# One tail as guest of the front parts, four tails behind the last front part with one loading of their weights

## The chip, the cores and the metric

One core of a Trainium2 chip runs the kernel. The metric is the device time of one execution in microseconds (us); of several runs the median stands. Matrix work runs on TensorE (PE; PEld is its loading of weights), elementwise work with reductions on VectorE (DVE), functions and copies on ScalarE (ACT), gathers are issued by GpSimd (POOL) and plain transfers by SyncE (SP). All transfers run on the same 16 DMA engines, here called the bus.

## The reference

One layer over 1024 tokens of 1024 features, all in float32:

```python
h = rmsnorm(x, norm_mix)
proj = h @ w_in                                    # parts for two token mixers
x = x + (g_gla * y_gla + g_swa * y_swa) @ w_out    # gated mixers, sliding window and linear attention
x = x + peer_ffn(rmsnorm(x, norm_ffn), ...)        # 8 heads x 16 of 16384 experts for each token
ple_gate = sigmoid(rmsnorm(x, norm_ple) @ w_ple_gate)
x = x + ple_gate * (p @ w_ple_proj)                # p: 256 features a token
return rmsnorm(x, norm_final)
```

In `peer_ffn` each head's query scores two lists of 128 keys; the 16 best pairs pick 16 experts. Of each expert a row u (1024) gives a dot product with the token, and, weighted by gelu of that and a softmax share, a row v (1024) is added up.

## The kernel before

The tokens are 8 tiles of 128. Three kinds of work run at once, woven by a plan of steps:

- **Rows.** Each tile has 8 heads x 16 experts = 128 rows. A row is one gather by GpSimd (line 596): for each of 128 tokens the u and v of its expert, 8 KB, 1 MB in all, into one of NS = 10 slots of the ring `uv`. VectorE takes the dot product (line 1354), ScalarE makes the weight (lines 1094, 1099), then either VectorE adds the weighted v (line 1382) or ScalarE makes a diagonal (line 1108) and TensorE adds it up in `ysum` (line 837); then the slot is free for the gather ten rows on. Step n (0 to 511) takes rows 2n and 2n + 1; every engine's program is a loop over the same steps and does its work in that order. From step 384 on (tiles 6 and 7) TensorE takes 3 of 4 rows, in tiles 3 to 5 every second; the first six rows of each tile are VectorE's. The top-16 searches of later heads run on VectorE 12 steps ahead.
- **Front parts.** SEGS = (1, 1, 2, 2, 2) tiles: norm, projections, mixers, output projection and queries of a segment, before its rows. Their weights are pieces of 1 MB (`slabs` in DRAM), loaded in order of use into a ring of RS = 3 places (`slab`, line 513), each when the piece three before has been used. The stages wq0 to wq8 are the queries (wq0 to wq7 use a piece each); with wq1 to wq8 VectorE runs `largest`, the 16 best of 128 for two lists of each tile.
- **Tails.** The per-layer embedding, the final norm and the output of a group of tiles, GROUPS = ((0, 1), (2, 3), (4, 5), (6,), (7,)). Stages: T0 (read-in of the tiles, sums of squares), gn (gain row), T1 (scale and turn), pg0 to pg3 (gate, one piece each), pp (embedding, one piece), mx, T2 (last norm, output). A tile's row sums are built in `acc[i % 2]`; when its rows are done, SyncE stores it to DRAM (`x2_d`, line 577), and T0's read-in (line 548) fetches the group back into `bufA`. Only the last tile's tail works in place, in `acc`.

The order is the list PLAN. `closing(s)` follows the last front stage of segment s with its queries wq2 to wq8, at `pace` steps each, woven with the opening of the next segment or with a tail: HOST = {0: 3, 1: 4} says that tail 0 is a guest of segment 3, and tail 1 of segment 4. So before, steps are: wq0 368, wq1 370, T0 of tail 1 at 372, wq2 374, then wq3 to wq8 every four steps to 400 with pg0 to pg3 and pp of tail 1 at 382 to 398 between them, T2 at 404; tail 2 from 407 to 425, tail 3 from 452 to 470, tail 4: pp 496, gn 498, the rest behind the rows, 514 to 521. SyncE issues all plain transfers in the order of the plan and waits, in that order, for what each needs; it runs ahead of the other engines as far as those waits let it.

Of the kernel before, what the change touches and what calls it, by code (L numbers as in the profile page):

```python
# [16 lines left out]
KT = D // P  # L17
# [18 lines left out]
TT = max(SEGS)  # L36
# [26 lines left out]
HOST = {0: 3, 1: 4}  # L63
# [67 lines left out]
def plan():  # L131

    found = []

    def stand(of, n, step):
        at = {name: at for at, o, name in found if o == of}
        step = max(step, found[-1][0] if found else step, at.get(BEHIND.get(n), step - 1) + 1)
        found.append((step, of, n))

    for s in range(NSEG):  # L140
        names = front_names(s)
        if not s or s - 1 in GUEST:
            names = OPENING + names
        due = DUE[s]
        last = len(names) - 1
        begin = found[-1][0] + 1 if found else due - last
        for i, n in enumerate(names):
            if n is not None:
                stand(s, n, begin + i * (due - begin) // last)
        pace = 2 if s in GUEST else 1 if s else 0.5  # L150
        for i, (of, n) in enumerate(closing(s)):
            stand(of, n, due + math.ceil(pace * (i + 1)))
    for q, tiles in enumerate(GROUPS):
        if q == LAST_GROUP:

            stand(q, "pp", PER_TILE * NTILE - 16)
            stand(q, "gn", PER_TILE * NTILE - 14)
            for i, n in enumerate(n for n in TAIL if n not in ("pp", "gn")):
                stand(q, n, END + 2 + i)
        elif q not in HOST:  # L160
            begin = max(found[-1][0] + 3, PER_TILE * (tiles[-1] + 1) + 4)
            for i, n in enumerate(TAIL):
                stand(q, n, begin + 2 * i)
    return found
# [110 lines left out]
for _, _s, _name in PLAN:  # L275
    if has_vector_part(_s, _name):
# [3 lines left out]

LOADS = [((s, n), n, USES_END[s, n] - (len(token_banks(SEGS[s])) if n[:2] == "wq" and n != "wq0" else 0))
         for _, s, n in PLAN if n in PIECES]
# [18 lines left out]
def build(nc, a, out):  # L301
    with ExitStack() as ctx:
# [59 lines left out]
        tp = [by_token_tile(bufC if q == LAST_GROUP else bufQ) for q in range(len(GROUPS))]  # L362
# [35 lines left out]
        x2 = [acc[:, (NTILE - 1) % 2:(NTILE - 1) % 2 + 1, :] if q == LAST_GROUP else x1 for q in range(len(GROUPS))]  # L398
# [62 lines left out]
        tail_out = sem("tail_out")  # L461

# [36 lines left out]
        def _(sp):  # L499
# [20 lines left out]
            def after_stage(at, s, n):  # L520
# [15 lines left out]
                if at == 0 and n == ("pp" if s == LAST_GROUP else "T0"):  # L536
                    tiles_of = GROUPS[s]
                    t0, tt = tiles_of[0], len(tiles_of)
                    if s in HOST:
                        sp.wait_ge(x1_out, 16 * WRITES[HOST[s] + 1])  # L540
                        sp.wait_ge(tile_set, SETS[HOST[s] + 1])
                        sp.wait_ge(vec_done, VEC_ORDER[HOST[s], "rt"])
                    else:
                        sp.wait_ge(tail_out, 16 * s)
                    if s != LAST_GROUP:
# [3 lines left out]
                    if s in HOST:  # L549
                        sp.wait_ge(bank_full, USES_END[HOST[s], f"va{last_batch(HOST[s])}"])  # L550
                    sp.dma_start(tpT[:, :, 0:tt * P], a["pT"][:, :, t0 * P:(t0 + tt) * P]).then_inc(tp_in, 16)
                    sp.dma_start(g_fin[0:1, :], a["g_fin"].unsqueeze(0)).then_inc(gfin_in, 16)
                if at == 2 and n == "T2":
# [12 lines left out]
            for n in range(FIRST, LAST + 3):  # L566
# [8 lines left out]
                if at == 0 and 1 <= i < NTILE:  # L575
# [26 lines left out]
        def _(pe):  # L602
# [17 lines left out]

            def turned(src, f0, tt):
# [20 lines left out]
            def by_token(src, tt):  # L642
                w = next_piece()
# [65 lines left out]
            def stage(s, n):  # L709
# [103 lines left out]
                elif kind == "pg":  # L813
                    if c == 0:
                        emptied_through(s, "T1")
                    by_token(thT, tt)
                elif n == "pp":
                    w = next_piece().rearrange("p k n -> p (k n)").rearrange("p (k n) -> p k n", k=2)
# [39 lines left out]
        def _(act):  # L858
# [77 lines left out]
            def stage(s, n):  # L936
# [120 lines left out]
                elif n == "T0":  # L1057
                    if s == LAST_GROUP:
                        act.wait_ge(x2_done, NTILE)
                    else:  # L1060
                        act.wait_ge(x2_in, 16 * (s + 1))
# [434 lines left out]
```

## Time and profile before

| | us |
|---|---|
| median of 3 runs | 3462.57 |
| lowest, highest | 3459.61, 3462.61 |
| the profiled execution, its own time | 3464.53 |
| its span, first to last instruction | 3462.6 |
| TensorE busy | 2831.6 (82%) |
| VectorE busy | 2525.6 (73%) |
| ScalarE, GpSimd busy | 1412.9 (41%), 1287.2 (37%) |
| moved by DMA | 1368.17 MB, mean 395 GB/s |

The shares are means over stages with different limits; they don't say which engine a stage waits for. Stretches are given in us from the span's start. A line of the timeline is start, duration, engine, line, what it writes and reads, and in brackets the engine's idle time before it with what ended it.

### The profile page before, as it was taken

To read this page: it belongs to the slowest core of one execution; us is meant where nothing else is said; L and a number is where in the kernel's file an instruction comes from. 1 tells how busy PE (TensorE), PEld (TensorE's weight loads), DVE (VectorE), ACT (ScalarE), POOL (GpSimd) and SP (SyncE) were. 2 spreads that over 40 slices of the span, in tenths; PEclk is the share of its full clock that TensorE was granted. 3 is DMA by queue.
4 is the path that set the end of the run, shared out by engine and by line. 5 is a ranking of instruction groups with operands and counts; after the bars stand their busy time and mean duration, and the time that the engine had idled before them with its cause. 6 is when DMAs were issued, how large, how long until landed. Compare 5 with 4: busy or idle time off the path is not lost.

```text
span 3462.6 us, 35613 instructions
## 1 busy us (share of the span) xinstructions
PE 2831.6 (82%) x11300; PEld 1912.9 (55%) x11300; DVE 2525.6 (73%) x5340; ACT 1412.9 (41%) x3593; POOL 1287.2 (37%) x1028
## 2 busy tenths in 40 slices
PE   8879769998978998876877969987896978758675
PEld 7877557765656865543644637655564645224223
DVE  0147658888878878788687996788778895776664
ACT  2324434445524344454343443444434444334332
POOL 0012223343442344443453443343334343544441
PEclk9999789999999999987988989999998998878887
DMA  7579999999999999999999999999999999999995
GB/s 243 201 302 419 370 383 421 421 421 420 420 419 388 392 421 421 420 412 414 411 422 409 411 400 421 421 421 417 399 410 420 413 399 418 408 421 422 421 422 213
DMA packets 193630, 1368.17 MB, mean 395 GB/s; under 512 B 22154, under 2 KB 24074, under 8 KB 29732
## 3 DMA queue, kind: packets, MB, share of 16 engines
q0 software_dynamic: 147456, 1073.81, 75.0%
q1 hardware_dynamic: 45988, 292.09, 21.2%
q8 instruction: 92, 1.51, 0.2%
q14 instruction: 94, 0.77, 0.1%
HBM read 1356.37 MB, written 9.44 MB: 394 GB/s over the span
## 4 chain that ended last, share of the span: by engine, by line
PE 37%; DMA 35%; DVE 12%; issue 7%; ACT 6%; POOL 2%; DVEq 0%; another core or an unknown queue 0%; POOLq 0%; SPq 0%; ACTq 0%
DMA uv<-in_uv,idx 30%; PE bank L639 12%; PE bank L649 11%; PE ysum L837 9%; DMA slab<-in_slabs 4%; DVE acc L1382 3%; DVE uv L1354 3%; POOL uv L596 2%; PE bank L706 1%; DVE lidx L1210 1%; ACT bufX L913 1%; DVE vals L1207 1%; DMA out<-bufA 1%; ACT dots L1099 1%; DVE bufE L1204 1%
## 5 line engine op out<-in xcount | busy, mean ns | idle before, releaser
L596 POOL DMA_INDIRECT uv<-in_uv,idx x1024 | 1287.0, 1257 | 2118.9 <-PE ysum L837 944.6
L1354 DVE SCALAR_TENSOR_TENSOR uv<-uv,hbuf 128x1024 f32<-128x1024 f32 x1024 | 1246.3, 1222 | 476.8 <-DMA uv<-in_uv,idx 457.2
L837 PE MATMUL ysum<-uv,diag 128*128 128x512 f32 x2092 | 1098.3, 670 | 373.2 <-ACT diag L1108 369.6
L837 PEld LDWEIGHTS ysum<-uv,diag 128*128 128x128 f32 x2092 | 427.0, 213 | 919.3 <-ACT diag L1108 471.1
L1382 DVE SCALAR_TENSOR_TENSOR acc<-uv,dots,acc 128x1024 f32<-128x1024 f32 x501 | 641.3, 1280 | 59.3 <-ACT dots L1099 42.3
L1094 ACT ACTIVATE dots<-dots 128x2 f32<-128x2 f32 x512 | 103.0, 201 | 1049.0 <-DVE uv L1354 1044.6
L639 PE MATMUL bank<-bufA,slab 128*128 128x256 f32 (+1 forms) x2400 | 439.9, 343 | 10.0 <-DMA slab<-in_slabs 9.4
L639 PEld LDWEIGHTS bank<-bufA,slab 128*128 128x128 f32 x2400 | 390.7, 195 | 72.6 <-issue 25.3
L649 PE MATMUL bank<-slab,bufA 128*128 128x256 f32 x1408 | 318.6, 385 | 5.7 <-DMA slab<-in_slabs 3.3
L649 PEld LDWEIGHTS bank<-slab,bufA 128*128 128x128 f32 x1408 | 270.6, 193 | 60.3 <-issue 16.4
L639 PE MATMUL bank<-bufC,slab 128*128 128x256 f32 (+1 forms) x1280 | 244.7, 353 | 21.4 <-ACT bufC L870 10.4
L1099 ACT ACTIVATE dots<-dots,gexp 128x1 f32<-128x1 f32 x1024 | 246.0, 287 | 20.6
L639 PEld LDWEIGHTS bank<-bufC,slab 128*128 128x128 f32 x1280 | 217.2, 203 | 61.2 <-issue 23.9
L1094 ACT ACT_TABLE_LOAD x160 | 205.3, 1283 | 2.9
L1108 ACT ACTIVATE diag<-ident,dots 128x128 f32<-128x128 f32 x523 | 196.6, 395 | 18.2 <-PE ysum L837 11.2
L870 ACT ACTIVATE bufE<-bank 128x512 f32<-128x512 f32 (+1 forms) x146 | 75.5, 523 | 289.1 <-PE bank L639 273.3
L649 PE MATMUL bank<-slab,bufC 128*128 128x256 f32 x512 | 120.5, 395 | 27.7 <-DVEq L1281 15.1
L649 PEld LDWEIGHTS bank<-slab,bufC 128*128 128x128 f32 x512 | 101.4, 199 | 50.5 <-DVEq L1281 16.7
L649 PE MATMUL bank<-slab,bufQ 128*128 128x256 f32 x512 | 120.9, 397 | 4.6 <-DMA slab<-in_slabs 3.9
L639 PE MATMUL bank<-bufQ,slab 128*128 128x256 f32 (+1 forms) x640 | 115.0, 338 | 7.8 <-DMA slab<-in_slabs 7.0
L649 PEld LDWEIGHTS bank<-slab,bufQ 128*128 128x128 f32 x512 | 102.4, 201 | 29.1 <-issue 7.3
L639 PE MATMUL bank<-bufB,slab 128*128 128x256 f32 (+1 forms) x640 | 118.4, 344 | 0.0
(160 smaller groups left out, 2303.6 us busy)
## 6 DMA issues: line engine op xcount, KB each, us to landing
slab<-in_slabs SPq DMA_DIRECT2D x255, 1024.0 KB
uv<-in_uv,idx POOLq DMA_INDIRECT x1024
x_d<-acc SPq DMA_DIRECT2D x7, 512.0 KB, 7.9
bufA<-in_x SPq DMA_DIRECT2D x3, 1024.0 KB, 11.6
bufA<-x_d SPq DMA_DIRECT2D x3, 1024.0 KB
out<-bufA SPq DMA_DIRECT2D x3, 1024.0 KB
bufQ<-in_x SPq DMA_DIRECT2D x2, 1024.0 KB, 16.6
x_d<-bufA SPq DMA_DIRECT2D x3, 512.0 KB, 7.7
```

What stands on the lines that cost most here:

```text
L596: nc.gpsimd.indirect_dma_start(out=uv[:, at % NS, :], out_offset=None, in_=a["uv"], in_offset=bass.IndirectOffsetOnAxis(ap=idx[:, g % 4, k ...
L639: m = mm(o, w[:, k, g * P:g * P + P], src(k), start=(k == 0), stop=(k == KT - 1))
L649: m = mm(b[:, c0:c0 + PW], src[:, k, t * P:t * P + P], w[:, k, :], start=(k == 0), stop=(k == KT - 1))
L706: m = mm(b[:, :, q], of[:, t, g * HD:g * HD + HD], pT[:, :, q], start=True, stop=True)
L837: ins = mm(ysum[:, c, :], diag[:, m % DS, :], uv[:, at % NS, D + c * 512:D + c * 512 + 512], start=(m == first), stop=(m == last))
L870: fn(dst, src, kw.pop("func", ACT.Copy), **kw).then_inc(emptied, 1)
L913: fn(probs[:, j, :], probs[:, j, :], ACT.Exp, bias=sm[:, 1, j:j + 1], accum_out=sm[:, 3, j:j + 1]).then_inc(window_exp, 1)
L1094: fn(part, part, ACT.Gelu_apprx_tanh).then_inc(gelu_done, 1)
L1099: m = fn(dots[:, g % 3, k:k + 1], dots[:, g % 3, k:k + 1], ACT.Copy, scale=gexp[:, g % 4, k:k + 1])
L1108: fn(diag[:, m % DS, :], ident[:], ACT.Copy, scale=dots[:, g % 3, k:k + 1]).then_inc(diag_done, 1)
L1354: v.scalar_tensor_tensor(out=row, in0=row, scalar=1.0, in1=hbuf[:, i % HB, :], op0=ALU.mult, op1=ALU.mult, accum_out=dots[:, g % 3, k:k + ...
L1382: v.scalar_tensor_tensor(out=row, in0=uv[:, at % NS, D:2 * D], scalar=dots[:, g % 3, k:k + 1], in1=row, op0=ALU.mult, op1=ALU.add).then_in ...
```

## The change

Tail 1 is no longer a guest of segment 4; the queries wq2 to wq8 of segment 4 follow each other every two steps, 372 to 384. Tail 1 runs after them, T0 at 387 to T2 at 405, pieces at 393 to 401; tail 2 runs from 408 to 426; tails 3 and 4 keep their steps. The five pieces of the tails (pg0 to pg3, pp) are loaded for tail 0 through the ring as before, and then once more, when the queries are done, into places that are free from then on: the three places of `slab`, `bufE` and `bufC`. Tails 1 to 4 use them from there. Tile 6, the only tile of its group, works in place in `acc` as tile 7 did, and is not stored to DRAM and read back. The last tail's embedding goes to the second half of `bufB` in place of `bufC`. The ring's list LOADS shrinks from 255 pieces to 235.

```diff
--- before.py
+++ after.py
@@ -60,7 +60,7 @@
 
 
 GROUPS = ((0, 1), (2, 3), (4, 5), (6,), (7,))
-HOST = {0: 3, 1: 4}
+HOST = {0: 3}
 GUEST = {h: q for q, h in HOST.items()}
 TAIL = ["T0", "gn", "T1", "pg0", "pg1", "pg2", "pg3", "pp", "mx", "T2"]
 LAST_GROUP = len(GROUPS) - 1
@@ -147,7 +147,7 @@
         for i, n in enumerate(names):
             if n is not None:
                 stand(s, n, begin + i * (due - begin) // last)
-        pace = 2 if s in GUEST else 1 if s else 0.5
+        pace = 2 if s in GUEST or s == NSEG - 1 else 1 if s else 0.5
         for i, (of, n) in enumerate(closing(s)):
             stand(of, n, due + math.ceil(pace * (i + 1)))
     for q, tiles in enumerate(GROUPS):
@@ -278,8 +278,14 @@
         VEC_ORDER[_s, _name] = _n
 
 
+FIRST_KEPT = len(HOST)
+KEPT = ["pg0", "pg1", "pg2", "pg3", "pp"]
+
+DIRECT = [q for q, tiles in enumerate(GROUPS) if len(tiles) == 1]
+
+
 LOADS = [((s, n), n, USES_END[s, n] - (len(token_banks(SEGS[s])) if n[:2] == "wq" and n != "wq0" else 0))
-         for _, s, n in PLAN if n in PIECES]
+         for _, s, n in PLAN if n in PIECES and not (n in KEPT and s >= FIRST_KEPT)]
 
 MOVED = [i for i in range(NTILE) if i not in AT]
 BATCHES = [sum(2 * t for t in SEGS[:s]) for s in range(NSEG + 1)]
@@ -359,7 +365,8 @@
         sqT = by_feature_tile(bufQ)
         yswT = by_feature_tile(bufQ)
         thT = by_feature_tile(bufQ)
-        tp = [by_token_tile(bufC if q == LAST_GROUP else bufQ) for q in range(len(GROUPS))]
+        tp = [by_token_tile(bufB)[:, 1:TT, :] if q == LAST_GROUP else by_token_tile(bufQ) for q in range(len(GROUPS))]
+        kept = [*(slab[:, i, :] for i in range(RS)), bufE[:], bufC[:]]
         HALF = 512 * TT
         loga = bufE[:, 0:HALF].rearrange("p (t n) -> p t n", t=TT)
         zs = bufE[:, HALF:2 * HALF].rearrange("p (t n) -> p t n", t=TT)
@@ -395,7 +402,7 @@
         uv = sb("uv", [P, NS, 2 * D])
         hbuf = sb("hbuf", [P, HB, D])
         acc = sb("acc", [P, 2, D])
-        x2 = [acc[:, (NTILE - 1) % 2:(NTILE - 1) % 2 + 1, :] if q == LAST_GROUP else x1 for q in range(len(GROUPS))]
+        x2 = [acc[:, tiles[0] % 2:tiles[0] % 2 + 1, :] if q in DIRECT else x1 for q, tiles in enumerate(GROUPS)]
         diag = sb("diag", [P, DS, P])
         vals = sb("vals", [P, LS, NH, 2, TOPK])
         lidx = sb("lidx", [P, LS, NH, 2, TOPK], U32)
@@ -459,6 +466,7 @@
         tp_in = sem("tp_in")
         gfin_in = sem("gfin_in")
         tail_out = sem("tail_out")
+        kept_in = [sem(f"kept_in{i}") for i in range(len(KEPT))]
 
         firsts = [(ident[:], a["ident"]), (g_mix[:], a["g_mix"])]
         consts = [(wga[:], a["wga"]), (wa2[:], a["wa2"]), (chunk_of[:], a["chunk_of"]), (tri[:], a["tri"]),
@@ -536,20 +544,28 @@
                 if at == 0 and n == ("pp" if s == LAST_GROUP else "T0"):
                     tiles_of = GROUPS[s]
                     t0, tt = tiles_of[0], len(tiles_of)
-                    if s in HOST:
-                        sp.wait_ge(x1_out, 16 * WRITES[HOST[s] + 1])
-                        sp.wait_ge(tile_set, SETS[HOST[s] + 1])
-                        sp.wait_ge(vec_done, VEC_ORDER[HOST[s], "rt"])
-                    else:
+                    host = HOST.get(s, NSEG - 1)
+                    if s <= FIRST_KEPT:
+
+                        sp.wait_ge(x1_out, 16 * WRITES[host + 1])
+                        sp.wait_ge(tile_set, SETS[host + 1])
+                        sp.wait_ge(vec_done, VEC_ORDER[host, "rt"])
+                    if s > 0:
                         sp.wait_ge(tail_out, 16 * s)
-                    if s != LAST_GROUP:
+                    if s not in DIRECT:
                         for t in tiles_of:
                             sp.wait_ge(x2_out[t % 2], 16 * (t // 2 + 1))
                         sp.dma_start(x2[s][:, 0:tt, :], x2_d[t0:t0 + tt].rearrange("t p d -> p t d")).then_inc(x2_in, 16)
-                    if s in HOST:
-                        sp.wait_ge(bank_full, USES_END[HOST[s], f"va{last_batch(HOST[s])}"])
+                    if s <= FIRST_KEPT:
+                        sp.wait_ge(bank_full, USES_END[host, f"va{last_batch(host)}"])
                     sp.dma_start(tpT[:, :, 0:tt * P], a["pT"][:, :, t0 * P:(t0 + tt) * P]).then_inc(tp_in, 16)
                     sp.dma_start(g_fin[0:1, :], a["g_fin"].unsqueeze(0)).then_inc(gfin_in, 16)
+                if at == 2 and (s, n) == (NSEG - 1, f"wq{NH}"):
+
+                    sp.wait_ge(bank_full, USES_END[s, n])
+                    sp.wait_ge(vec_done, VEC_ORDER[s, n])
+                    for place, name, landed in zip(kept, KEPT, kept_in):
+                        sp.dma_start(place, a["slabs"][PIECES.index(name)]).then_inc(landed, 16)
                 if at == 2 and n == "T2":
                     sp.wait_ge(vec_done, VEC_ORDER[s, "T2"])
                     t0, tt = GROUPS[s][0], len(GROUPS[s])
@@ -572,7 +588,7 @@
                         sp.wait_ge(x2_out[i % 2], 16 * (i // 2))
                     sp.dma_start(acc[:, i % 2, :], x1_d[i]).then_inc(acc_in[i % 2], 16)
                 i, at = divmod(n - 3, PER_TILE)
-                if at == 0 and 1 <= i < NTILE:
+                if at == 0 and 1 <= i <= GROUPS[DIRECT[0]][0]:
                     sp.wait_ge(x2_done, i)
                     sp.dma_start(x2_d[i - 1], acc[:, (i - 1) % 2, :]).then_inc(x2_out[(i - 1) % 2], 16)
                 for at in range(3):
@@ -618,6 +634,13 @@
                 pe.wait_ge(slab_in[n % RS], 16 * (n // RS + 1))
                 return slab[:, n % RS, :].rearrange("p (k n) -> p k n", k=KT)
 
+            def tail_piece(s, n):
+                if s < FIRST_KEPT:
+                    return next_piece()
+                i = KEPT.index(n)
+                pe.wait_ge(kept_in[i], 16)
+                return kept[i].rearrange("p (k n) -> p k n", k=KT)
+
             def turned(src, f0, tt):
                 for f in range(f0, f0 + 4, 2):
                     for gs in feature_banks(tt):
@@ -639,8 +662,8 @@
                             m = mm(o, w[:, k, g * P:g * P + P], src(k), start=(k == 0), stop=(k == KT - 1))
                     m.then_inc(bank_full, 1)
 
-            def by_token(src, tt):
-                w = next_piece()
+            def by_token(src, tt, w=None):
+                w = next_piece() if w is None else w
                 for ts in token_banks(tt):
                     b = bank_for()
                     for t in ts:
@@ -813,9 +836,9 @@
                 elif kind == "pg":
                     if c == 0:
                         emptied_through(s, "T1")
-                    by_token(thT, tt)
+                    by_token(thT, tt, tail_piece(s, n))
                 elif n == "pp":
-                    w = next_piece().rearrange("p k n -> p (k n)").rearrange("p (k n) -> p k n", k=2)
+                    w = tail_piece(s, n).rearrange("p k n -> p (k n)").rearrange("p (k n) -> p k n", k=2)
                     pe.wait_ge(tp_in, 16 * (s + 1))
                     for q in range(2):
                         for t in range(tt):
@@ -1055,8 +1078,8 @@
                     for q in range(2):
                         copied(row[:, q * 512:q * 512 + 512], full())
                 elif n == "T0":
-                    if s == LAST_GROUP:
-                        act.wait_ge(x2_done, NTILE)
+                    if s in DIRECT:
+                        act.wait_ge(x2_done, GROUPS[s][0] + 1)
                     else:
                         act.wait_ge(x2_in, 16 * (s + 1))
                     square_sums(junk_t0, [(x2[s][:, t, :], stat_t[:, 0, t:t + 1]) for t in range(tt)])
```

## Rows read from the trace of the kernel before

**Rows 1.** the profile page: DMA queues, with packets, MB and share of the 16 engines' span

```profile
q0 software_dynamic: 147456, 1073.81, 75.0%
q1 hardware_dynamic: 45988, 292.09, 21.2%
```

**Rows 2.** busy us (and records) of PE, PEld, DVE, ACT, POOL in a stretch, PEclk, DMA share, GB/s

```profile
2623.10:2729.80 106.70, 86.80 (x314) 58.85 (x313) 88.31 (x250) 42.18 (x106) 44.77 (x35) 0.87 1.01 419
2729.80:2756.80 27.00, 20.78 (x79) 15.07 (x78) 26.44 (x71) 8.89 (x24) 9.99 (x8) 0.94 0.99 397
2756.80:2837.80 81.00, 72.38 (x237) 42.47 (x235) 69.27 (x194) 33.70 (x86) 33.75 (x30) 0.99 0.98 398
2837.80:2974.00 136.20, 103.35 (x297) 57.41 (x298) 92.98 (x173) 69.95 (x165) 57.86 (x44) 0.87 1.00 410
2974.00:3239.60 265.60, 178.58 (x362) 77.12 (x361) 183.98 (x347) 99.62 (x272) 118.34 (x99) 0.83 1.01 421
3239.60:3413.00 173.40, 122.71 (x216) 47.56 (x214) 117.80 (x214) 51.95 (x169) 81.46 (x65) 0.84 1.01 422
...
2878.90:2959.90 81.00, 80.44 (x262) 48.06 (x262) 55.72 (x104) 43.31 (x104) 40.82 (x31) 1.00 0.99 405
1081.00:1107.00 26.00, 25.69 (x105) 17.02 (x104) 25.16 (x97) 12.90 (x32) 10.03 (x9) 1.00 1.01 409
1112.40:1130.70 18.30, 18.30 (x75) 14.41 (x74) 13.13 (x47) 2.71 (x10) 3.75 (x4) 0.91 0.81 300
```

**Rows 3.** stretches again, only line 1354 (dot products): DVE busy (records)

```profile
2623.10:2729.80 106.70, 39.21 (x64) 0.87 1.01 419
2756.80:2837.80 81.00, 34.23 (x56) 0.99 0.98 398
```

**Rows 4.** timeline of SP and PE: tile 6's store, the last tail's pieces; start, us, instruction

```profile
3092.72 0.32 SPq L577 DMA_DIRECT2D x_d<-acc  x1
...
3435.90 16.29 PE L649 MATMUL bank<-slab,bufQ 128*128 128x256 f32 x64 [0.72 <-ACT bufQ L899]
...
3441.86 0.33 SPq L513 DMA_DIRECT2D slab<-in_slabs  x1
```

**Rows 5.** line 1207 (MAX8 of the queries' scores) in 2623.1 to 2729.8

```profile
L1207 DVE MAX8 vals<-bufE x32: 273/276/296, 2636.1 to 2728.2; 128x8 f32<-128x128 f32 x32
```

**Rows 6.** timeline of DVE, one call of `largest` and what follows

```profile
1088.75 0.86 DVE L1207 MAX8 vals<-bufE 128x8 f32<-128x128 f32 x4
...
1094.23 1.23 DVE L1354 SCALAR_TENSOR_TENSOR uv<-uv,hbuf 128x1024 f32<-128x1024 f32 x1 [0.18 <-DVE lidx L1210]
```

**Rows 7.** timeline of SP: the read-ins of tails 1 and 2, the store of tile 5

```profile
2617.75 0.38 SPq L548 DMA_DIRECT2D bufA<-x_d  x1
...
2736.01 0.33 SPq L577 DMA_DIRECT2D x_d<-acc  x1
...
2856.40 0.37 SPq L548 DMA_DIRECT2D bufA<-x_d  x1
```

**Rows 8.** timelines of ACT, DVE and POOL around T0 of tail 2; in brackets the idle time

```profile
2867.72 1.06 ACT L877 ACTIVATE bufQ<-bufA 128x1024 f32<-128x1024 f32 x1 [14.47 <-DMA bufA<-x_d]
...
2871.68 0.17 DVE L1143 RECIPROCAL stat_t<-stat_t 128x2 f32<-128x2 f32 x1 [15.25 <-ACT stat_t L881]
...
2876.05 1.36 POOL L596 DMA_INDIRECT uv<-in_uv,idx  x1 [20.79 <-PE ysum L837]
```

**Rows 9.** DMA queues in 2870 to 2880, columns as in rows 1

```profile
q1 hardware_dynamic: 564, 3.26, 79.8%
q0 software_dynamic: 118, 0.83, 21.5%
```

**Rows 10.** groups of PE in 2883.4 to 2951.6: busy us, mean ns, idle before

```profile
L837 PE MATMUL ysum<-uv,diag 128*128 128x512 f32 x73 | 32.5, 592 | 0.0
L649 PE MATMUL bank<-slab,bufQ 128*128 128x256 f32 x128 | 28.3, 379 | 0.0
```

## The prediction

> **What bounds the kernel now.** I read the page's queue table first, then busy time by stretch, then the timeline around single events. The two DMA queues together keep the 16 engines busy for 96% of the span [rows 1], and where nothing is in the way the bus moves 422 GB/s (stretch F below, [rows 2]). One gather or one weight load is 1,048,576 bytes, so 2.49 us of bus; a step has two gathers, 4.97 us. Adding bytes would cost time almost everywhere, but the bus is not the only limit near the front parts: over steps 391 to 427 it moves 398 and 410 GB/s (C and D below, [rows 2]), and in 2878.9 to 2959.9, where a tail of two tiles runs alone, TensorE is busy for 80.4 of 81.0 us [rows 2]. The question for each load removed is therefore whether the bus or something else sets the pace where it stood.
>
> I cut the time after step 370 into stretches whose edges are starts of dot products, two per step: A steps 370 to 385, B 386 to 390, C 391 to 404, D 405 to 427, E 428 to 475, F 476 to 509, then the last tail. The count in [rows 3] confirms the steps: each dot product leaves two records, so x64 is 16 steps.
>
> **Bytes.** Before, five tails load five pieces each, 25 loads. After, ten: five for the guest, five kept. Fifteen loads fewer: five of tail 2 (all in D), five of tail 3 and three of tail 4 in E, one of tail 4 in F, one behind the last gather. That last one is hidden: it is issued at 3441.86 under a run of TensorE that goes from 3435.90 for 16.29 us without a gap [rows 4], so I price it at 0; were TensorE to wait for it, it would be 2.5. Tile 6 also no longer goes out to DRAM (0.5 MB at 3092.72 [rows 4]) and back (a tail's read-in, half the size): 2.5 us of bus, in E.
>
> **E and F.** TensorE works 178.6 of 265.6 us and 122.7 of 173.4, VectorE 184.0 and 117.8 [rows 2], so the bus decides and bytes turn into time: E loses eight loads (19.9) and 2.5, so 22.4 us; F loses 2.5. If the shorter tails meet a little idle time of the bus, E gives 19.
>
> **A: the queries of the last front part, now one every two steps.** Before, A holds four calls of `largest` for two tiles: 32 MAX8, eight each [rows 5]. After, wq1 to wq8 all fall there, eight calls. One call takes 5.3 us of VectorE (from the first MAX8 at 1088.75 to 1094.05, 0.18 before the next dot product at 1094.23, [rows 6]). VectorE's work in A goes from 88.3 [rows 2] to 88.3 + 4 x 5.3 = 109.5 us, against a bus need of 16 x 4.97 + 6 x 2.49 = 94.5 and TensorE, which gives up two pieces and some turning of the guest tail and takes three pieces of queries at 7.1 us [rows 10] with their score products, some 93. VectorE becomes the bound. The nearest row where queries of two tiles come every two steps is 1081.0 to 1107.0: four steps in 26.0 us, VectorE at 25.16, 97% [rows 2]. So A takes 109.5 / 0.97 = 113, and 114 with the first pair of steps, where no landed rows are in store yet: +7.3 against 106.7. Bounds 109.5 (no idle time) and 120 (a wait for ScalarE of 1 us in each of seven stages besides).
>
> **B: the burst, and the wait for the residual rows.** SyncE now issues the five kept loads only when VectorE has done wq8 (step 385), then waits for `x2_done` 6, stores tile 5 and only then reads in tiles 2 and 3 for tail 1. Before, that read-in left at 2617.75, four steps ahead of T0 [rows 7]; nobody waited for it. In front of it now stand 5 x 2.49 + 1.25 us and its own 2.49: 16.2 us of bus. The ring of ten rows is full of landed rows at the end of A (VectorE was the slow one), and lets only four more gathers out before ScalarE stands at T0: 10.0 us. All of it is bus-bound, so the rows land some 26 us after the first dot product of step 386. From the landing the trace has a case, T0 of tail 2: ScalarE goes on at 2867.72 after 14.47 us of waiting, VectorE at 2871.68 after 15.25, GpSimd issues its next gather at 2876.05 after 20.79 [rows 8], and the dot product two steps later that begins the row of 81.0 us stands at 2878.9, 11.2 behind the landing. So 26 + 1 + 11 = 38 us for B, against 27.0: +11. What is queued behind ScalarE's wait: the weights of rows 776 on, their diagonals, so TensorE's sums, so the slots of the ring. Bounds: 29 if the gathers stand behind the whole burst and the ring's store hides more of it (16.2 + 1 + 11.2), and 45 if each byte ahead of the read-in shares the bus with a gather (2 x 16.2 + 1 + 11.2).
>
> On such sharing, the Trainium skill's page "DMA: Bandwidth & Descriptors" (section on queues, rings and completion order) says that each engine takes turns between the rows of queues that have work, a packet at a time; by it B would lie at its upper bound, 45, and the whole sum at -2, if gathers never ran out. In the trace a side that has nothing to send leaves the bus to the other: in 2870 to 2880 q1 has 79.8% and q0 21.5% [rows 9]. My sum goes by what is there to be moved.
>
> **C: tail 1 alone.** Its twin in the trace is tail 2, 2878.9 to 2959.9: the same instructions on two tiles with the same three rows in two steps on TensorE, 81.0 us for 14 steps, TensorE 80.4. In its dense part, 2883.4 to 2951.6, the four pieces cost TensorE 28.3 us, 7.1 each, and the row sums 32.5 [rows 10]. The bus would need 14 x 4.97 = 69.6. So C is TensorE's: I take 80, against 81.0 before, though two loads fewer are in it. Bounds 74 (the ring lets dot products run two rows further ahead and the next stall absorbs it) and 82.
>
> **D: tail 2.** Five loads fewer are 12.4 us of bus. But three of them filled a hole: during T0's wait gathers stop, and from 2870 to 2880 q0 moves 0.83 MB where the bus could move 4.2 [rows 9]; the missing 3.4 MB are 8 us. The wait itself hangs on a store and a read-in, which stay. The other two stood where TensorE is saturated. I take 134.5 against 136.2; bounds 125 (the loads' 12.4 nearly whole) and 137.
>
> **Sum.** A +7.3, B +11.0, C -1.0, D -1.7, E -22.4, F -2.5, end 0: -9.3 us. The profiled execution took 3464.5, of which 3462.6 are span; it becomes 3455.2. The median of the runs is 3462.57, so 3453.3.
>
> **Rivals.** (1) *The bus sets the time everywhere.* Then A to C keep their bytes and D gives all: 22.4 + 2.5 + 12.4 = 37.3, median 3425. For it: the bus at or near 1.0 in every row of [rows 2]. Against it: VectorE's 109.5 us of work in A, and TensorE's row of 81.0. The skill's "Perfetto Trace Analysis" (Identifying the Most-Contended Engine) holds that matmul busy time is a bad metric and weight loads' busy share a good one; by it TensorE would have room in C and D, which is this rival. The trace shows 48.1 of 81.0 for the weight loads in that row, yet the matmuls follow each other with 0.6 us of gaps, so I give it 0.12. (2) *Half way:* the ring absorbs more of TensorE's backlog, C 74 and D 127: 13.5 us better, median 3440. 0.18. (3) *The burst costs more:* B 45 and A 119 make -9.3 + 7 + 5 = +2.7, median 3465, no change that can be told. 0.20. (4) *Slower: the stages of queries are paced by the chain of TensorE, ScalarE and VectorE,* not by VectorE's work. Place: steps 372 to 385, each wq waiting for its copies. Price: steps 123 and 124, where TensorE is crowded by pieces, took 18.3 us with VectorE only 13.1 of it busy [rows 2]; seven pairs at 18.3 in place of 14.2 are +29, median 3482. It decides from 16.5 us a pair on ((9.3 + 6.9) / 7 above 14.2). Against it: 1081.0 to 1107.0, with no wait in it. 0.08. (5) That the loads are not saved: the counts in the code say 255 before and 235 plus five after; no chance of its own.
>
> **Numbers.** Forecast 0.42. A measurement of this kernel can tell about 0.2%, 6.9 us, from no change, and my forecast lies only 2.4 us beyond that: two thirds of its chance are faster, one third the same. Faster: 0.12 + 0.18 + 0.27 = 0.57; same 0.15 + 0.17 = 0.32; slower 0.08 + 0.03 = 0.11. The range 3432 to 3472 takes in the forecast with its bounds and rivals 2 and 3, and leaves out 1 and 4, 0.20.
>
> **What would show it.** In the changed profile: 64 MAX8 between the dot products of steps 370 and 386 and VectorE at 95% or more there, in 114 us; a wait of ScalarE for the read-in of tiles 2 and 3 of about 10 us (step 388), with hardly a gather moving behind it; TensorE at 99% while tail 1 runs, with a bus below 370 GB/s; a hole of some 8 us after T0 of tail 2; and E shorter by 22. The prediction is wrong if VectorE has room in A, if tail 1 runs at 5 us a step, or if E gives less than 19.

## The result and the profile after

The changed kernel takes 3467.14 us, median of 18 runs, against 3461.89 for the kernel before, also of 18. The ratio is 1.0019 with a 95% interval of 1.0012 to 1.0027, so some 6.6 us slower; in a second set of runs (after_again below) it was 1.0013 (1.0000 to 1.0025), 4.5 us. I had forecast 3453.3, 9.3 us faster. The time lies inside the stated range of 3432 to 3472, but the sign is the other.

The page of the kernel after, against [rows 1] and the table ahead of the prediction:

```profile
span 3465.2 us, 35599 instructions
...
DMA packets 191182, 1351.40 MB, mean 390 GB/s; under 512 B 21882, under 2 KB 23802, under 8 KB 29204
...
q0 software_dynamic: 147456, 1073.81, 75.4%
q1 hardware_dynamic: 43540, 275.31, 20.0%
```

The bytes are gone as foreseen: 1368.17 MB less 1351.40 is 16.8 MB, 15 loads and twice 0.5 MB. The mean rate went from 395 to 390 GB/s. What was saved in bytes, 40 us of bus at 422 GB/s, came back as idle time of the bus.

Busy time by stretch after (PE, PEld, DVE, ACT, POOL, then PEclk, DMA share, GB/s), cut at the same dot products as [rows 2]: A, B, C, D, E, F and the last tail.

```profile
2624.40:2740.80 116.40, 88.01 (x361) 62.84 (x359) 108.09 (x379) 30.98 (x91) 40.20 (x35) 0.92 0.94 378
2740.80:2783.10 42.30, 7.29 (x12) 2.91 (x12) 21.47 (x39) 9.21 (x23) 8.23 (x6) 0.53 0.74 302
2783.10:2864.60 81.50, 79.42 (x260) 47.66 (x259) 54.08 (x100) 43.10 (x104) 38.12 (x31) 1.00 0.95 374
2864.60:3003.00 138.40, 103.87 (x299) 57.57 (x298) 93.22 (x172) 72.51 (x165) 57.30 (x48) 0.87 0.94 367
3003.00:3245.00 242.00, 167.53 (x358) 73.13 (x356) 183.41 (x347) 98.45 (x271) 120.25 (x95) 0.85 1.01 420
3245.00:3415.90 170.90, 118.09 (x216) 45.33 (x216) 117.78 (x214) 52.11 (x170) 83.00 (x66) 0.88 1.01 421
3415.90:3465.20 49.30, 24.81 (x80) 17.13 (x80) 15.26 (x18) 13.33 (x29) 0.00 (x0) 0.71 0.11 44
```

The reader is to see three things. In A VectorE works 108.1 of 116.4 us, against 88.3 of 106.7 before. In B nearly everything rests, TensorE works 7.3 of 42.3 us, and the bus is at 302 GB/s. In C TensorE is at 79.4 of 81.5 with the bus at 374. From E on the bus is full and the stretches are shorter.

| us | before | forecast | after | again |
|---|---|---|---|---|
| A, steps 370 to 385 | 106.7 | 114 | 116.4 | 116.7 |
| B, 386 to 390 | 27.0 | 38 | 42.3 | 42.4 |
| C, 391 to 404 | 81.0 | 80 | 81.5 | 81.5 |
| D, 405 to 427 | 136.2 | 134.5 | 138.4 | 136.4 |
| E, 428 to 475 | 265.6 | 243.2 | 242.0 | 243.3 |
| F, 476 to 509 | 173.4 | 170.9 | 170.9 | 170.9 |
| A to F against before | | -9.3 | +1.6 | +1.3 |

"Again" is a second profile of the changed kernel, below. The profiles thus account for some 1.5 us of the 4.5 to 6.6 that the ratios show. The rest I could not place. Up to step 370 all kernels here have the same steps, and that dot product began anywhere between 2616.5 and 2624.5 us in their single profiles. Stretches within a profile are steadier than that, and I argue from them.

### The profile page after: what moved, and what is told of

The parts are those of the page before. It is cut to its first block, busy times and chain, and to the rows that moved or that the text cites. A ratio compares the mean times of both kernels' runs of the same rounds, so it can differ in the third digit from the quotient of the medians.

```text
span 3465.2 us, 35599 instructions
## 1 busy us (share of the span) xinstructions
PE 2809.6 (81%) x11300; PEld 1902.5 (55%) x11300; DVE 2524.1 (73%) x5340; ACT 1413.8 (41%) x3594; POOL 1289.0 (37%) x1028
## 2 busy tenths in 40 slices
DMA packets 191182, 1351.40 MB, mean 390 GB/s; under 512 B 21882, under 2 KB 23802, under 8 KB 29204
## 4 chain that ended last, share of the span: by engine, by line
DMA 34%; PE 33%; DVE 16%; issue 8%; ACT 6%; POOL 2%; DVEq 0%; POOLq 0%; ACTq 0%; SPq 0%
DMA uv<-in_uv,idx 30%; PE bank L662 11%; PE bank L672 10%; PE ysum L860 9%; DVE acc L1405 4%; DVE uv L1377 4%; DMA slab<-in_slabs 3%; POOL uv L612 2%; DVE lidx L1233 2%; PE bank L729 1%; DVE vals L1230 1%; DMA bufA<-x_d 1%; ACT bufX L936 1%; DVE bufE L1227 1%; DMA out<-bufA 1%
## 5 line engine op out<-in xcount | busy, mean ns | idle before, releaser
L860 PE MATMUL ysum<-uv,diag 128*128 128x512 f32 x2092 | 1079.3, 660 | 406.8 <-ACT diag L1131 404.9
L860 PEld LDWEIGHTS ysum<-uv,diag 128*128 128x128 f32 x2092 | 419.3, 209 | 942.4 <-issue 482.3
L1131 ACT ACTIVATE diag<-ident,dots 128x128 f32<-128x128 f32 x523 | 196.9, 395 | 22.2 <-PE ysum L860 15.1
L662 PEld LDWEIGHTS bank<-bufQ,slab 128*128 128x128 f32 x640 | 103.7, 195 | 23.3 <-DMA slab<-in_slabs 8.3
L662 PEld LDWEIGHTS bank<-bufB,slab 128*128 128x128 f32 x640 | 105.8, 197 | 18.7 <-issue 8.4
## 6 DMA issues: line engine op xcount, KB each, us to landing
out<-bufA SPq DMA_DIRECT2D x3, 1024.0 KB, 11.6
```

What stands on the lines that cost most here:

```text
L662: m = mm(o, w[:, k, g * P:g * P + P], src(k), start=(k == 0), stop=(k == KT - 1))
L860: ins = mm(ysum[:, c, :], diag[:, m % DS, :], uv[:, at % NS, D + c * 512:D + c * 512 + 512], start=(m == first), stop=(m == last))
L1131: fn(diag[:, m % DS, :], ident[:], ACT.Copy, scale=dots[:, g % 3, k:k + 1]).then_inc(diag_done, 1)
```

## The experiments

Theory 1 is that of the prediction: VectorE bounds A, the wait for the read-in of tail 1 makes B, TensorE bounds C and most of D, and only E and F turn bytes into time.

**early_readin.** The wait alone is taken away.

```diff
+                if (s, n) == (1, "T0"):
+                    return
+                if at == 0 and (s, n) == (NSEG - 1, "wq1"):
+                    s, n = 1, "T0"
                 if at == 0 and n == ("pp" if s == LAST_GROUP else "T0"):
```

> Undoes one thing of the changed kernel: the read-in of tiles 2 and 3 for tail 1 (with its embeddings and gain row) is issued at step 370, ahead of the five kept loads, as it was before the change. Theory 1 (ScalarE's wait for the read-in behind 7 MB of transfers makes stretch B, steps 386 to 390, long): B falls from 42.3 us to about 32 (five steps of gathers, 24.9, and what of the five loads and the store the full ring does not cover), A gets some 3 us longer as it now moves the 1.25 MB; the whole is 8 to 12 us faster than the changed kernel, so about 3457. Rival (the burst of five loads itself holds the gathers up, whoever waits): B stays above 40 and the whole at 3467.

Measured: 3456.68 us, ratio 0.9977 (0.9968 to 0.9986). A, B, C and D of this kernel:

```profile
2617.90:2737.80 119.90, 92.77 (x363) 64.87 (x361) 108.30 (x377) 30.96 (x91) 41.68 (x35) 0.90 0.95 380
2737.80:2762.50 24.70, 11.21 (x22) 4.75 (x23) 21.50 (x40) 11.52 (x30) 10.75 (x9) 0.66 1.01 424
2762.50:2848.90 86.40, 76.98 (x249) 47.40 (x248) 54.02 (x98) 41.00 (x96) 36.17 (x28) 0.94 0.94 365
2848.90:2990.60 141.70, 106.49 (x298) 57.59 (x297) 93.16 (x171) 72.23 (x165) 57.75 (x48) 0.85 0.91 356
```

B fell by 17.6 us, more than expected. The burst still stands in B and takes bus from the gathers, which move 4.9 MB there (5.5 MB of other transfers beside them) against 7.1 MB in the kernel before; that the landed rows in the ring hide this is my reading of it. A took 3.5 us back, as expected, C 4.9 and D 3.3, which I had not expected, so that A to F together are 4.6 us shorter, while the medians differ by 8 to 10. Theory 1 stands for B: without the wait the burst doesn't make it long. The rival, B above 40 whoever waits, falls.

**half_search.** `largest` looks only for the first 8 of 16 in the last segment; which experts tiles 6 and 7 take is changed by it.

```diff
-                for c in (slice(0, 8), slice(8, 16)):
+                for c in (slice(0, 8), slice(8, 16))[:1 if s == NSEG - 1 else 2]:
```

> The changed kernel with the second half of the top-16 search left out for the last segment's queries (indices 8 to 15 of its lists stay those of an earlier tile): VectorE has some 2.7 us less work in each of eight calls, the gathers move as many bytes. Theory 1 (VectorE bounds A, steps 370 to 385): VectorE's work there falls from 108 to some 87 us and A from 116.4 us to about 98, what the bus and TensorE need; the ring is then not full at its end, so B grows by some 5: the whole is 10 to 15 us faster, about 3454. Rival (the chain of TensorE, ScalarE and VectorE paces the queries): A stays above 110 and the whole within 4 us of the changed kernel.

Measured: 3456.72 us, ratio 0.9988 (0.9979 to 0.9997). A and B:

```profile
2622.10:2720.80 98.70, 86.33 (x363) 63.60 (x361) 83.64 (x219) 31.43 (x91) 42.98 (x35) 0.97 1.01 421
2720.80:2770.90 50.10, 7.30 (x11) 3.04 (x12) 21.49 (x39) 8.98 (x23) 8.26 (x6) 0.52 0.75 307
```

A is 98.7 where 98 was expected, and bus-bound at 421 GB/s: VectorE was the bound, no chain of engines. B grew by 7.8 (some 5 were expected), in my reading because the ring now brings no landed rows into it; the net in A and B is 9.9, and the whole 10.4 us faster than the changed kernel, as expected.

**half_gates.** Half of the contraction of the gate products is left out in tails 1 and 2 (`by_token` is given the number of blocks to sum over).

```diff
-                    by_token(thT, tt, tail_piece(s, n))
+                    by_token(thT, tt, tail_piece(s, n), KT // 2 if s in (1, 2) else KT)
```

> The changed kernel with half of the gate products (contraction over 4 of 8 blocks) left out in tails 1 and 2: TensorE has 3.5 us less in each of eight stages, bytes are the same. Theory 1 (TensorE bounds C and D, where the tails run alone): C, steps 391 to 404, falls from 81.4 us to 71 to 74 (the bus needs 69.6), D, 405 to 427, from 138.4 to some 128; the whole about 18 to 20 us faster, 3448. Rival (C and D are long for the waits between the tails' stages, not for TensorE's work): C falls by less than 4 us, the whole by less than 8.

Measured: 3453.41 us, ratio 0.9977 (0.9967 to 0.9986). C and D:

```profile
2782.60:2856.50 73.90, 67.66 (x199) 35.62 (x197) 54.93 (x99) 43.75 (x104) 42.01 (x33) 1.00 1.00 414
2856.50:2988.60 132.10, 92.75 (x231) 45.33 (x232) 92.92 (x171) 72.08 (x165) 59.38 (x45) 0.83 0.95 389
```

C is 7.6 us shorter and near the bus's need, D 4 to 6 (10 was expected), the whole 13.7 (18 to 20 were expected). TensorE is the bound of C, and only a part of D's length.

**two_guests.** The other part of the change alone.

```diff
-HOST = {0: 3}
+HOST = {0: 3, 1: 4}
```

> The other part of the change alone: tail 1 stays a guest of segment 4 as before the change (queries every four steps), and only tails 2, 3 and 4 use kept weights, loaded once after the last query at step 400; tile 6 in place. Ten loads fewer than before in place of fifteen, and the store and read-in of tile 6 gone. Theory 1: A and B are as in the kernel before (106.7 and 27.0 us), C too; D moves the same five loads as before, now ahead of tail 2; E is 22 to 23 us shorter and F 2.5. So 20 to 25 us faster than before, about 3439, and 28 faster than the changed kernel. Rival (the saving of bytes behind step 428 is given back by something that the in-place tail or the kept places bring): no faster than 3455.

Measured: 3445.62 us, ratio 0.9950 (0.9936 to 0.9964), 17 us faster than the kernel before where 20 to 25 were expected. A is 105.7, B 26.9, E 243.5, F 170.8, all as expected; but C and D:

```profile
2757.10:2843.80 86.70, 72.96 (x240) 42.98 (x238) 69.61 (x196) 37.23 (x93) 34.06 (x30) 0.98 0.98 398
2843.80:2984.40 140.60, 106.18 (x297) 58.05 (x298) 92.46 (x171) 66.51 (x160) 53.95 (x43) 0.84 0.95 381
```

Together 227.3 us against 217.2 before, with the same five loads in them. In the kernel before these stood behind tail 2's read-in (2857.9 to 2912.4); here they stand ahead of it, at step 402. That gave theory 2: where ScalarE waits and gathers can't be issued, loads cost nothing, and neither do they where TensorE is the bound; the same loads elsewhere are paid for.

**two_late.** two_guests with the burst moved behind that read-in.

```diff
                     sp.dma_start(g_fin[0:1, :], a["g_fin"].unsqueeze(0)).then_inc(gfin_in, 16)
-                if at == 2 and (s, n) == (NSEG - 1, f"wq{NH}"):
-
-                    sp.wait_ge(bank_full, USES_END[s, n])
-                    sp.wait_ge(vec_done, VEC_ORDER[s, n])
...
+                    if s == FIRST_KEPT:
+                        sp.wait_ge(bank_full, USES_END[NSEG - 1, f"wq{NH}"])
+                        sp.wait_ge(vec_done, VEC_ORDER[NSEG - 1, f"wq{NH}"])
+                        for place, name, landed in zip(kept, KEPT, kept_in):
+                            sp.dma_start(place, a["slabs"][PIECES.index(name)]).then_inc(landed, 16)
```

> two_guests with one thing moved: the five kept loads are issued behind the read-in of tail 2 (step 407) in place of step 402. Theory 2 (loads that stand in the hole of tail 2's T0 and in the stretch where TensorE is the bound cost nothing, and the same bytes ahead of the tail are paid for): C (391 to 404) and D (405 to 427), 86.6 and 140.7 us in two_guests, go back to about 81 and 136 to 138, as in the kernel before, and the whole falls by 6 to 10 us, to about 3438. Rival (C and D are longer in two_guests for another reason, such as where the kept places lie): no change within 3 us, 3445.

Measured: 3437.24 us, ratio 0.9928 (0.9915 to 0.9942), the fastest kernel of the study, 25 us faster than the kernel before. C and D:

```profile
2749.10:2831.50 82.40, 72.14 (x228) 41.21 (x226) 69.42 (x195) 33.45 (x86) 35.92 (x30) 0.97 0.96 394
2831.50:2968.50 137.00, 102.89 (x298) 57.22 (x299) 92.89 (x173) 70.43 (x167) 56.19 (x45) 0.87 0.99 407
```

The order of the same transfers alone brought C and D from 227.3 to 219.4 us, 8 of the 12.4 us of bus that the five loads need. ScalarE's wait for the read-in did not get shorter by it, 15.8 us against 12.3 in two_guests, so the gain is that the loads go through while it waits and behind it, as theory 2 has it. Which of its two places, the hole or the stretch of TensorE, takes them for nothing, this run can't tell; two_best_late below bears on it.

**one_late.** The same move in the changed kernel: the five loads behind the read-in of tail 1. The edit is that of two_late.

> The changed kernel with the five kept loads issued behind the read-in of tail 1 (step 387) in place of ahead of it. Theory 2 (bytes ahead of the read-in lengthen ScalarE's wait, and bytes behind it fill the hole in which no gather can be issued): the read-in lands some 12 us sooner, B falls from 42.3 to 29 to 33 us, the zero bus of 11 us in it goes, C stays at 81 to 84; the whole falls by 8 to 12 us to about 3457, as far as with early_readin. Rival (tail 1 then waits for its pieces, which land only 12 us after the read-in): C grows by what B loses, the whole stays at 3467.

Measured: 3459.23 us, ratio 0.9987 (0.9978 to 0.9996). B is 33.3 us and C 81.3. Against the changed kernel's 3467.14 us that is 7.9 us faster, against its 3464.84 of the same set of runs 5.6; A to F together are 5.1 to 5.4 shorter. The hole of B, first in the changed kernel (GpSimd's gathers, then the queue's row of the DMA view for 2775.8 to 2783.1, the only queue with packets), then in one_late (the same, 2765.1 to 2772.5):

```profile
2753.01 0.96 POOL L612 DMA_INDIRECT uv<-in_uv,idx  x1 [0.30 <-issue]
2780.34 1.73 POOL L612 DMA_INDIRECT uv<-in_uv,idx  x1 [26.36 <-PE ysum L860]
...
q0 software_dynamic: 15, 0.12, 11.3%
```

```profile
2751.39 0.96 POOL L611 DMA_INDIRECT uv<-in_uv,idx  x1 [0.30 <-issue]
2769.62 1.82 POOL L611 DMA_INDIRECT uv<-in_uv,idx  x1 [17.27 <-PE ysum L859]
...
q1 hardware_dynamic: 432, 3.15, 102.4%
```

Gathers rest for 26.4 us in the one and for 17.3 in the other, and the hole that stays is filled by q1, the kept loads. ScalarE's wait is 12.4 us in place of 21.4. B and C are as expected; of the 8 to 12 us expected for the whole, 5.6 to 7.9 came. D is 141.0, 3 to 5 above the changed kernel, as it was in early_readin. In both the bus stands still twice behind T0 of tail 2, for 2.6 and 3.5 us here and 3.6 and 3.4 in early_readin, where the changed kernel has one such hole of 2.6; why there are two when tail 1 comes through sooner stays open.

**two_state.** two_late, with the tiles of tail 2 read into the memory of `state` at step 387, so that T0 of tail 2 waits for no output of tail 1.

```diff
+        x2[2] = state[:].rearrange("p a h n -> p a (h n)")
...
                     sp.dma_start(x2_d[i - 1], acc[:, (i - 1) % 2, :]).then_inc(x2_out[(i - 1) % 2], 16)
+                    if i == GROUPS[2][-1] + 1:
...
+                        sp.dma_start(x2[2], x2_d[4:6].rearrange("t p d -> p t d")).then_inc(x2_in, 16)
```

> two_late, and tail 2 has its tiles in the memory of state, which is free once the last front part is through: they are read in at step 387, and T0 of tail 2 waits for no output of tail 1. Theory: ScalarE's wait of 14.5 us at that T0, with 20 us without a new gather, goes; D falls from some 137 to 122 to 128 (the bus needs 114 for the gathers and 12 for the kept loads), the whole to 3424 to 3430. Rival (TensorE, which works 103 us of D's 136, takes its time anyway, as the wait only shifted its work): D falls by less than 4 us.

Measured: 3450.06 us, ratio 0.9965 (0.9954 to 0.9976), a miss: 13 us slower than two_late. SyncE's queue, then who waited for the front part's pieces in 2752 to 2800:

```profile
2732.02 0.33 SPq L595 DMA_DIRECT2D x_d<-acc  x1
2740.52 0.38 SPq L601 DMA_DIRECT2D state<-x_d  x1
2740.94 39.75 SPq L522 DMA_DIRECT2D slab<-in_slabs  x5
...
PE bank L680 <- DMA slab<-in_slabs: 14.7, 1, 14.7
```

SyncE stood 8 us for the store of tile 5 before it could read it in, and the pieces of weights behind it in its queue came late: the first left 15.1 us after the first dot product of step 386, against 6.6 in two_late, with 1 MB more ahead of it. TensorE waited 14.7 us, C went to 94.4. D was 135.5, only 1.5 below two_late; that TensorE and the five loads took what the stall gave back is argued, not shown.

**early_state.** The same with one guest, on early_readin.

> early_readin (one guest, as in the changed kernel) with the tiles of tail 2 in the memory of state, read in at step 387: neither tail waits for a read-in. Theory: D falls from 141.7 to 125 to 130, C stays at 86 (bursts ahead, then TensorE), A at 119; the whole is 12 to 16 us faster than early_readin, about 3443, and still slower than two_state by 15, as the crowded queries (A) are paid. Rival (with no read-in to wait for, one guest and two guests come out the same): within 4 us of two_state.

Measured: 3445.84 us, ratio 0.9949 (0.9936 to 0.9963). A 120.4, B 24.2, and C and D:

```profile
2765.70:2852.80 87.10, 77.93 (x251) 47.86 (x250) 54.10 (x97) 41.02 (x96) 37.09 (x28) 0.94 0.94 375
2852.80:2980.80 128.00, 106.65 (x298) 58.53 (x297) 93.63 (x171) 72.54 (x165) 55.67 (x48) 0.91 0.97 385
```

D fell by 13.7 here, within the expectation, and the whole by 11 against early_readin (12 to 16 were expected). The 13.7 us are what the wait at T0 costs where no loads are left to fill it. "Slower than two_state by 15" was wrong: it is 4 us faster, since two_state lost its time in SyncE's queue.

**two_best** and **two_best_late.** two_state with the read-in at step 398, behind the front part's pieces; the kept loads at step 402 in the one, behind step 407 in the other.

```diff
+                if at == 0 and (s, n) == (1, "pp"):
...
+                    sp.dma_start(x2[2], x2_d[4:6].rearrange("t p d -> p t d")).then_inc(x2_in, 16)
```

> two_guests (five kept loads at step 402), with the tiles of tail 2 in the memory of state, read in at step 398: late enough that SyncE doesn't hold up the pieces of the front part behind it, as it did in two_state (C 94.4 us). Theory: C 86 to 89 and D 126 to 129 as in early_state, so 4 to 6 us faster than two_late: 3432. Rival (the wait at T0 only shifted TensorE's work): D stays at 135 and the whole at 3440 or above.

> two_best with the five kept loads behind step 407, as in two_late. No hole is left for them to fill there, so they are paid in D: C 82 to 84, D 135 as in two_state; the whole at 3438 to 3441, 5 or more slower than two_best. Rival (loads late are better whatever stands around them): faster than two_best.

Measured: 3447.05 us (0.9959, 0.9945 to 0.9972) and 3441.22 us (0.9936, 0.9921 to 0.9950). C and D of the two:

| us | C | D |
|---|---|---|
| two_late | 82.4 | 137.0 |
| two_best | 89.8 | 135.3 |
| two_best_late | 84.3 | 135.5 |

My expectation of D (126 to 129) fell, and the rival of two_best held: without the wait D is only 1.5 us shorter. Why it is not 128 as in early_state is not shown. It has more to move, 3.4 MB beside the gathers in two_best and 6.6 in two_best_late against 1.3, and the bus is full (418 to 422 GB/s) for the first 58 us of both; but two_best has only 2.1 MB more, worth 5 of the 7 us. Loads late were better than early again (5.5 us in C, nothing in D), which the rival of two_best_late had said and I had not. Here ScalarE has no read-in to wait for, so a gain of this kind, 6 of the 8 us of two_late, doesn't need a hole. In the 40 us in which TensorE works without a gap the bus moves 418 GB/s in two_best_late and 379 in two_best; that this slack takes up the bytes is again a reading and not shown by a run of its own.

One comparison more. In two_best (two guests) and early_state (one guest, five loads fewer) neither tail waits for a read-in, and both have the kept loads ahead of the tail that uses them first. They come out equal: 3447.05 and 3445.84 us, A to F 773.2 and 773.7. The crowded queries of early_state cost 14 us in A, and B, C and D give 13 of them back.

**pace3.** The changed kernel with the last queries every three steps.

```diff
-        pace = 2 if s in GUEST or s == NSEG - 1 else 1 if s else 0.5
+        pace = 2 if s in GUEST else 3 if s == NSEG - 1 else 1 if s else 0.5
```

> The changed kernel with the last segment's queries every three steps (wq8 at 391) in place of two; tails 1 and 2 stand seven steps later, T0 at 394 and 415. Theory 1 (VectorE's bound in A is what the crowding costs): from 370 on, three steps hold one call of the search: VectorE 18.9 us, bus 17.4, so the time over the bus's need falls from 12 us in all to some 6, and the whole is 4 to 7 us faster than the changed kernel, 3461; the wait for the read-in of tail 1 stays at some 20 us. Rival (the chain paces the queries): the pairs stretch to the same length per query, 14 us, and three steps of gathers fit in it, which would give more than 10 us.

Measured: 3465.05 us, ratio 1.0010 (0.9998 to 1.0022), some 2 us below the changed kernel and not to be told from it; 4 to 7 were expected. Steps 370 to 392, with all eight calls of `largest` in them (64 MAX8), took 146.3 us at 397 GB/s, as long as these steps took in the kernel before (146.7), so the crowding went; but steps 393 to 397 took 46.5. Steps 370 to 434 take 413.7 us in all against 414.9 in the changed kernel. That the wait at T0 now meets a ring without landed rows, as in half_search, would explain the 46.5; it is not shown.

**after_again.** The changed kernel once more.

> The changed kernel as it is, on the chip of this group, for its stretches a second time: A 116, B 42, C 81, D 138, E 242 us, each within 2, and a ratio to the kernel before of 1.001 to 1.003.

Measured: 3464.84 us, ratio 1.0013 (1.0000 to 1.0025); the stretches stand in the table above, each within 2 us of what was expected.

## Why the prediction was wrong

**The bytes, E and F: right.** E -23.6 and -22.3 (forecast -22.4), F -2.5 (-2.5), the last tail unchanged within 0.4 (0).

**A: right in kind, 2.4 to 2.7 us short.** VectorE's work was sized at 109.5 us and measured 108.1. It waited 5.0 us for gathers at the start, where I had allowed 1, and 108.1 / 0.97 + 5.0 = 116.4. So VectorE was busy for 93% of A and not the 95 that I had named as a sign. In [rows 5] stood 32 MAX8; now 64, and hardly a wait between them:

```profile
L1230 DVE MAX8 vals<-bufE x64: 268/275/296, 2637.3 to 2739.2; 128x8 f32<-128x128 f32 x64
...
DVE uv L1377 <- DMA uv<-in_uv,idx: 5.0, 2, 3.7
```

**B: the term with the largest miss, 4.3 us, and the step that failed.** The prediction's step "the rows land some 26 us after the first dot product of step 386" measured 30.7, and "11.2 behind the landing" measured 11.6. Against [rows 7, 8]:

```profile
2740.78 1.28 SPq L568 DMA_DIRECT2D slab<-in_slabs  x3
2742.10 0.44 SPq L568 DMA_DIRECT2D bufE<-in_slabs  x1
2742.58 0.44 SPq L568 DMA_DIRECT2D bufC<-in_slabs  x1
2746.99 0.33 SPq L593 DMA_DIRECT2D x_d<-acc  x1
2747.55 0.38 SPq L558 DMA_DIRECT2D bufA<-x_d  x1
...
2771.49 1.06 ACT L900 ACTIVATE bufQ<-bufA 128x1024 f32<-128x1024 f32 x1 [21.44 <-DMA bufA<-x_d]
```

The order is the one that was foreseen, loads, store, read-in, and ScalarE waited 21.4 us where I had expected 10. The term mis-sized is that of the gathers ahead of the landing: in 2740.8 to 2775.8 q0 moved 5.59 MB, 5.3 gathers and not 4. GpSimd did issue four before it had to rest, but some issued in A still had to land, which the prediction had left out. The way the bytes shared the bus was nearer to the upper bound (45) than to the sum: while both queues had work, in 2751 to 2767, they moved about as much each:

```profile
q0 software_dynamic: 497, 3.68, 54.8%
q1 hardware_dynamic: 487, 3.07, 46.4%
```

ScalarE also came to T0 sooner, 9 us into B and not some 16, which makes its wait longer but not B.

**C: 81.5 for 80.** The twin row's 81.0 us were the time to take; the us less has no row behind it. TensorE was busy for 97% of C (99 forecast), with the bus at 374 GB/s (below 370 forecast).

**D: no gain where I took one.** I took -1.7 for five loads fewer; it was +0.2 and +2.2, above the bound of 137 in one of the two profiles, which are 2 us apart themselves. The reason that I gave for so small a gain, the hole and TensorE's bound, was right (two_late against two_guests: the same loads cost 8 us where they stand in neither), but then the loads there cost nothing, and the term is 0 or above. The bus idles for it: 367 GB/s in D after, 410 before. The hole is there, after T0 of tail 2: the bus moves 271 GB/s in 2905.1 to 2923.3, some 6.5 us of it missing where I had said 8.

**The sum.** A, B, C and D missed by +2.4, +4.3, +1.5 and +3.9 us, E by -1.2, together +10.9; in the second profile +2.7, +4.4, +1.5, +1.9 and +0.1, together +10.6. All but D in the first profile lie inside the bounds that I had stated for them, and all four on the slow side of what I took: each time I had left out a small cost (the first gathers of A, the ones in flight at the start of B, the last us of C, and that loads in D are worth nothing). By the ratios the whole missed by 13.8 to 15.9 us, so 3 to 5 are not placed. A forecast 2.4 us beyond what can be told from no change could not carry that.

**The rivals.** Rival 1 (the bus everywhere, 3425) is refuted by half_search and half_gates: less work for VectorE and for TensorE at the same bytes made the kernel faster. The rule of the Trainium skill that I had set beside it ("Perfetto Trace Analysis", Identifying the Most-Contended Engine), taken as a test of which engine sets the time, did not hold in C: weight loads were busy in 47.7 of 81.5 us, and yet TensorE was the bound. The same page (Optimization Strategy) says that a kernel whose most-contended engine changes over time may gain by interleaving these stretches; this case agrees in A, which is 10 us longer without TensorE's tail between VectorE's queries (13 in early_readin), but not in the whole: with neither tail waiting, the woven two_best and the unwoven early_state come out equal, with five loads more in the woven one. Rival 2 (C 74 and D 127, 3440) is refuted by C 81.5 and D 138.4. Rival 3 (the burst costs more: B 45, A 119, together 3465) came nearest in the whole, but partly by luck: A and B gave 6.7 of its 12 us, and C and D, which it had left as forecast, gave 5.4 more. Rival 4 (the chain paces the queries) fell in half_search.

## What to carry to other kernels

Before counting removed bytes as time, look at where they stand: in E and F each megabyte gave its 2.4 us, in D five loads gave nothing. Where an engine must wait for a transfer and holds up the bus's main stream by it, put that transfer first in its queue and the ones that nobody waits for yet behind it: this order alone was worth 8 us in two_late and 5 to 8 in one_late, and 6 in two_best_late, where no wait was left. And take a change of several parts apart: loading the weights once, with tile 6 in place, was worth 17 us (two_guests; 25 with the loads late, two_late), and putting tail 1 behind the queries took all 17 away again, and some 5 more. About half of that was the wait for its read-in (early_readin, 8 to 10 us), the other half went when tail 2 waited for no read-in either (early_state, 11 us), and then the woven order was worth no more than the five loads that it adds (two_best).

## What the runs showed of the hardware

A ring of ten gathers hides a stop of its consumers only as far as its rows reach: after the one at 2753.01 no gather was issued for 26.4 us, and the bus then stood still for 11.1 us (2771.7 to 2782.8). While two queues had work, they shared the bus about evenly (3.7 and 3.1 MB in 16 us); when one had none, the other had all of it (q1 with 102.4% of the bus in one_late). SyncE's one queue carries waits further than they are meant: 8 us for the landing of a 0.5 MB store, and 1 MB read in behind it, became 14.7 us of TensorE waiting for a piece of weights that had nothing to do with them.
